# The row of inverse norms: spread over the partitions by way of DRAM instead of by TensorE

## The reference

```python
def rmsnorm(x, g):
    y = x * lax.rsqrt(mean(x * x, -1) + EPS)
    return y * g
x = x + 0.5 * ((silu(rmsnorm(x, g1) @ w_gate) * (rmsnorm(x, g1) @ w_up)) @ w_down)
...
x = rmsnorm(x, final_norm)
# Fox: q, k, v, f_logit, gate = split(x @ w_in)
# log_f = log_sigmoid(f_logit + b_f); cum = cumsum(log_f)
# scores = q k^T * scale + cum_q - cum_k, causal softmax, times v, times silu(gate), @ w_out
```

## Time and profile before

| | |
|---|---|
| time, median of 3 runs | 717.7 us (717.63 to 717.78) |
| profiled execution: its own time | 716.91 us |
| profiled execution: its span | 715.1 us |
| TensorE busy | 704.1 us, 98% |
| VectorE busy | 484.5 us, 68% |
| ScalarE busy | 377.9 us, 53% |
| GpSimd busy | 57.9 us, 8%, 33 instructions |
| granted TensorE clock, mean | 0.998 |

### The profile page before, as it was taken

How to read it: one execution, slowest core, us unless ns; L and a number is a source line. 1 busy time by engine, 2 the same in 40 slices (tenths; PEclk the granted TensorE clock), 3 DMA queues, 4 the chain that set the end, 5 groups by cost and what they waited for, 6 DMA issues and landing times.

```text
span 715.1 us, 9717 instructions
## 1 busy us (share of the span) xinstructions
PE 704.1 (98%) x3724; PEld 595.6 (83%) x3724; DVE 484.5 (68%) x726; ACT 377.9 (53%) x515; POOL 57.9 (8%) x33
## 2 busy tenths in 40 slices
PE   8999999999999999999999999999999999999995
PEld 7888888888887778888888888888888888877884
DVE  5797777755476446777767755566766737798756
ACT  6865545444377645754445644477444624575450
POOL 0000000000001300000000000000006442141001
PEclk9999999999999999999999999999999999999999
DMA  8996555555355323655455555435573183543001
GB/s 292 371 353 260 203 190 176 181 207 201 119 201 210 119 69 138 243 200 203 176 176 185 207 213 222 176 138 216 193 257 133 38 316 125 176 166 124 1 1 59
DMA packets 21731, 129.33 MB, mean 181 GB/s; under 512 B 2584, under 2 KB 4384, under 8 KB 7488
## 3 DMA queue, kind: packets, MB, share of 16 engines
q1 hardware_dynamic: 20160, 127.38, 49.3%
q10 hardware_dynamic: 1488, 1.34, 0.6%
q0 software_dynamic: 48, 0.13, 0.0%
HBM read 127.79 MB, written 1.06 MB: 180 GB/s over the span
## 4 chain that ended last, share of the span: by engine, by line
PE 96%; DVE 1%; ACT 1%; DMA 1%; issue 0%; DVEq 0%; ACTq 0%
PE ps L398 26%; PE ps L378 16%; PE ps L380 15%; PE ps L379 15%; PE ps L402 13%; PE ps L389 1%; PE ps L594 1%; PE ps L937 1%; PE ps L416 1%; PE ps L390 1%; PE ps L766 1%; ACT whi L1011 1%; DMA sm<-in_sm 1%; PE ps L471 0%; PE ps L917 0%; PE ps L927 0%
## 5 line engine op out<-in xcount | busy, mean ns | idle before, releaser
L398 PE MATMUL ps<-xt,whi 128*128 128x512 f32 x796 | 201.3, 393 | 0.0
L1443 DVE TENSOR_TENSOR wlo<-raw,whi 128x2048 fp32r<-128x2048 f32 x69 | 159.0, 2313 | 38.7 <-ACT whi L1011 38.5
L1011 ACT ACTIVATE whi<-raw 128x2048 fp32r<-128x2048 f32 x78 | 148.6, 1908 | 48.9 <-PE ps L380 46.9
L398 PEld LDWEIGHTS ps<-xt,whi 128*128 128x128 f32 x796 | 142.9, 189 | 25.0
L378 PE MATMUL ps<-whi,xt 128*128 128x512 f32 (+1 forms) x304 | 121.9, 401 | 0.1
L380 PE MATMUL ps<-whi,xt 128*128 128x512 f32 (+1 forms) x304 | 117.0, 385 | 0.0
L379 PE MATMUL ps<-wlo,xt 128*128 128x512 f32 (+1 forms) x304 | 116.8, 384 | 0.0
L402 PEld LDWEIGHTS ps<-xt,wlo 128*128 128x128 f32 x796 | 109.1, 190 | 8.0
L402 PE MATMUL ps<-xt,wlo 128*128 128x256 f32 x796 | 111.5, 282 | 0.0
L1396 POOL TENSOR_TENSOR wlo<-raw,whi 128x2048 fp32r<-128x2048 f32 (+1 forms) x9 | 41.3, 4586 | 554.6 <-ACT whi L1011 554.6
L1055 ACT ACTIVATE work<-ps 128x512 f32<-128x512 f32 x44 | 26.2, 597 | 96.8 <-PE ps L398 96.6
(11 more groups left out here) (218 smaller groups left out, 674.4 us busy)
## 6 DMA issues: line engine op xcount, KB each, us to landing
raw<-in_gu SPq DMA_DIRECT2D x41, 1024.0 KB, 4.8
raw<-in_dn SPq DMA_DIRECT2D x22, 1024.0 KB, 4.7
raw<-in_win SPq DMA_DIRECT2D x8, 1024.0 KB, 4.7
raw<-in_fqk SPq DMA_DIRECT2D x8, 1024.0 KB, 4.8
raw<-in_wout SPq DMA_DIRECT2D x4, 1024.0 KB, 5.0
raw<-in_fg SPq DMA_DIRECT2D x4, 1024.0 KB, 4.8
raw<-in_fv SPq DMA_DIRECT2D x4, 1024.0 KB, 4.7
raw<-in_fo SPq DMA_DIRECT2D x4, 1024.0 KB, 4.8
```

Source lines behind the costliest of these rows:

```text
L398: return pe.matmul(ps[:, bank, :], wh[:, w[i]], x, start=ks[i] == 0, stop=ks[i] == KD - 1)
L1011: act.activation(whi[:, c % RING, 0:n], raw[:, c % RING, 0:n], ACT.Copy).then_inc(hi_ready, 1)
L1443: dve.tensor_tensor(wlo[:, c % RING, 0:n], raw[:, c % RING, 0:n], whi[:, c % RING, 0:n].bitcast(F32), ALU.subtract).then_inc(lo_ready, 1)
```

## The change

The diagonals, the products with ones and the copies from PSUM are gone, with all their waits, and the identity's wait on TensorE moves to behind the first pair of chunks. In their place GpSimd waits for the scales, stores them to DRAM as one row of 256 (pieces of 4 bytes, 128 partitions x 2), waits for that store, and reads the row back on all 128 partitions (1 KB each). It does so for the first feed-forward in front of its other work, for the second feed-forward and for Fox behind the chunks of the mixer's output. VectorE waits for the landed row in the places where it waited for the copy, but in both feed-forwards it prepares the second chunk (`lo(C_GU[f] + 1 + RING)`) ahead of the wait and not behind the first hidden product.

```diff
 # TensorE
-            def rstd_to_row(i, bank, diagonal):
-                pe.wait_ge(eye_landed, 16)
-                pe.wait_ge(diag_ready, 2 * i + 2)
-                for t in range(NT):
-                    m = pe.matmul(ps[:, bank, t * P:(t + 1) * P], ones, diagonal[:, t, :], start=True, stop=True)
-                m.then_inc(row_psum, 1)
...
-                            if static and j == 0 and i == 3 and u == 1:
-                                pe.wait_ge(row_ready, f + 1)
...
                 if f == 0:
                     first_pair()
+                    pe.wait_ge(eye_landed, 16)
                 for i in range(2 * (1 - f), 4):
                     gate_and_up(0, i)
-                    if f and i == 1:
-                        rstd_to_row(f, ROW, ffn_diag)
...
-                    if nb and not half:
-                        rstd_to_row(2, 7, diag)
...
                 if h == 1:
                     pe.wait_ge(f_order, 1)
-                    pe.wait_ge(row_ready, 3)
 # ScalarE
-            def row(i, bank, dst):
-                act.wait_ge(row_psum, i + 1)
-                act.activation(dst, ps[:, bank, 0:S], ACT.Copy).then_inc(row_ready, 1)
 # GpSimd
+            def spread_rstd(i, norms, row):
+                pool.wait_ge(rstd_ready, norms)
+                pool.dma_start(rstd_rows[i].rearrange("(t p) -> p t", p=P), rstd, allow_slow_non_contiguous=True).then_inc(rstd_stored, 16)
+                pool.wait_ge(rstd_stored, 16 * (i + 1))
+                pool.dma_start(row, rstd_rows[i].partition_broadcast(P)).then_inc(row_landed, 16)
...
-            for c in [C_WOUT + 1, C_WOUT + 2] + list(range(C_FO, C_DQ)):
+            spread_rstd(0, 1, ffn_row)
+            for c in (C_WOUT + 1, C_WOUT + 2):
+                lo(c)
+            spread_rstd(1, 3, ffn_row)
+            spread_rstd(2, 4, rstd_row)
+            for c in range(C_FO, C_DQ):
                 lo(c)
 # VectorE
-            def diagonal(i, dst):
-                dve.wait_ge(rstd_ready, i + 2 if i else 1)
-                for t in range(NT):
-                    dve.tensor_scalar(dst[:, t, :], ident, rstd[:, t:t + 1], None, ALU.mult).then_inc(diag_ready, 1)
...
                     norm(0)
-                    dve.wait_ge(eye_landed, 16)
-                    diagonal(0, ffn_diag)
                 lo(C_GU[f] + RING)
                 if f:
                     sum_halves(0, 1)
-                dve.wait_ge(row_ready, f + 1)
+                lo(C_GU[f] + 1 + RING)
+                dve.wait_ge(row_landed, 16 * (f + 1))
                 times_row(0, 0)
                 times_row(0, 1)
                 hidden(0, 1, 0)
-                lo(C_GU[f] + 1 + RING)
...
-            dve.wait_ge(row_ready, 3)
+            dve.wait_ge(row_landed, 48)
```

More of the change, by code:

```diff
@@ L64 @@
 N_CHUNKS = C_DO + 4
-DOWN, ROW = 4, 7
+DOWN = 4
 WF_LO = 32
@@ L160, in build @@
         ffn_row = view(work, NG * S + 4 * S, S)
-        ffn_diag = view(work, NG * S + 5 * S, S, "p (t k) -> p t k", t=NT)
         x_turned = view(work, 7700 - KD * S, KD * S, "p (k s) -> p k s", k=KD)
@@ L192, in build @@
         bias2 = gains[:, 1:4, :].rearrange("p a c -> p (a c)").rearrange("p (h k) -> p h k", h=H2)
-        diag = view(work, 6144, 256, "p (t k) -> p t k", t=NT)
         rstd_row = view(work, 6400, 256)
@@ L261, in build @@
             sem(n) for n in ("f_psum", "f_order", "f_neg", "f_soft", "f_log", "cum_ready", "f_rest", "cum_spread"))
-        diag_ready, row_psum, row_ready = sem("diag_ready"), sem("row_psum"), sem("row_ready")
+        rstd_stored, row_landed = sem("rstd_stored"), sem("row_landed")
+        rstd_rows = nc.dram_tensor("rstd_rows", (3, S), F32, kind="Internal").ap()
         gate_ready = sem("gate_ready")
@@ L390, in both_halves, with tile_sums @@
                 return pe.matmul(*small, start=False, stop=False)
-            def tile_sums(bank, wh, wl, u, ks, middle=None):
+            def tile_sums(bank, wh, wl, u, ks):
                 w = [slice(k * S + u * P, k * S + (u + 1) * P) for k in ks]
@@ L404, in tile_sums @@
                     m = high(i)
-                    if middle and i == 2:
-                        middle()
                 return m
@@ L523, in gate_and_up @@
                         for u in range(2):
-                            if static and j == 0 and i == 3 and u == 1:
-                                pe.wait_ge(row_ready, f + 1)
-                            row = (lambda: rstd_to_row(0, ROW, ffn_diag)) if static and j == f == u == 0 and i == 3 else None
-                            m = tile_sums(2 * i + u, wh, wl, u, range(KD), row)
+                            m = tile_sums(2 * i + u, wh, wl, u, range(KD))
                     m.then_inc(chunk_used, 1)
@@ L1068, in ffn @@
                     hi(C_GU[f] + RING)
-                    row(f, ROW, ffn_row)
                     load_table(ACT.Silu)
@@ L1229, in _ @@
                 if nb == 0:
-                    row(2, 7, rstd_row)
                     act.wait_ge(f_psum, 1)
@@ L1679, in _ @@
             norm(2)
-            diagonal(1, ffn_diag)
             dve.wait_ge(wf_hi, 1)
@@ L1690, in _ @@
             norm(3)
-            diagonal(2, diag)
             lo(C_FG + RING)
```

## The result

| | before | after |
|---|---|---|
| time, median of 5 runs each on one chip | 717.63 us (717.51 to 717.78) | 729.04 us (727.56 to 729.77) |
| ratio of the times | | 1.0158, 95% interval 1.0146 to 1.0169 |
| profiled execution: own time / span | 716.91 / 715.1 us | 729.77 / 727.6 us |
| granted TensorE clock, mean | 0.998 | 0.990 |

A forecast was written before the change was run, and what follows sets the result against it. TensorE's own work bounds the kernel (704.1 of 715.1 us busy, 96% of the chain). Removed rows save 0.43 + 0.45 + 0.44 = 1.32 us, everything else counts 0: 717.7 to 716.4 us, range 715.8 to 719.8 us.

The forecast's parts named there:

- What do the two transfers take?: First feed-forward: store and read of the row take 4.1 us each, so the row lands at 33.8 us, no stall.
- The limit: First feed-forward: the row may land as late as 34.5 us, 9.15 us after the scales, without TensorE stalling.
- my bounds: Per transfer, 2.0 us (output stores) to 11.2 us (x loads queued behind other loads); ends: no stall or 13 us.
- Rival A: First feed-forward: store and read each wait for chunk loads ahead; stall 6.3 us, time 722.7 us; chance 0.17.
- Every microsecond beyond T = 34.5 is a microsecond of TensorE: First feed-forward, T being when the row has landed: each microsecond past 34.5 us costs TensorE one microsecond.
- The sign that the prediction named for A or B: First feed-forward: VectorE's first scaling starts after 34.5 us and TensorE idles for the difference behind VectorE's subtraction.
- Rival B: First feed-forward: slower transfers, or GpSimd shut out by VectorE, cause a small stall; 717.9 or 719.0 us; chance 0.17.
- Fox ... 10 us of slack: Fox: row lands at 484.4 us, its first user is needed at 494.5, so TensorE never waits: 0 us.
- what the steps said: Removing the row products saves TensorE 0.43 us (first feed-forward), 0.45 us (second) and 0.44 us (Fox).
- rival C: All three places: each row also broke the weight-load stream; 0.55 us a row, 1.65 us saved, 716.05 us; chance 0.08.
- T + 6.7 us: First feed-forward: chunk 6 is ready for TensorE 6.7 us after the row has landed.
- T may be 306 to 307 us, 18 us after the scales: Second feed-forward: the row may land this late without TensorE stalling; with 8.4 us for the transfers, 0 us.

## Why the prediction was wrong

**The step that failed** is "What do the two transfers take?", and in it the store: "I take 4.1 us for both". The store takes 11.1 to 11.5 us in all three places, the read 6.1 to 6.4. In the first feed-forward that is 17.8 us from scales to row and not 8.4: 7.0 us more for the store, 2.0 for the read, 0.4 for hand-offs. The limit was 9.15 us for everything, so the store alone breaks it. The nearest rows that I chose, the identity and the small parameters, are loads of longer pieces into SBUF; no store of 4-byte neighbours was in the trace, and even the end of my bounds, 11.2 us, was taken from a row with another cause. I held both transfers to the lower part of the bounds with no row for it but likeness, and gave a late row only 0.34 in all. Where the bounds are 2.0 and 11.2 us a transfer and the limit of 4.5 us each lies between them, the chance of a stall was to be taken nearer to a half.

**The Trainium skill.** "DMA: Bandwidth & Descriptors" ("Anatomy of one DMA — SWDGE (gpsimd) path") gives some 2.0 us of fixed cost; here no transfer on GpSimd's queue took less than 3.2 us, and the read alone has a median of 5.5. The same page ("Rules for kernel authors") warns of one descriptor for each element. The warning was right in its sign, and I priced it at nothing. Its ground is not what the runs show: with half as many elements the store took 9.9 to 11.3 us, with as many lying apart 5.6 to 5.9. Its "Specifications" name 512 bytes as the least transfer for full rate; 64-byte pieces took 5.8 us here and 512-byte ones 5.2 (medians), so that bound does not separate the slow stores from the quick ones in this case.

**Rival A** had the right sign and place, and its way to the price ("Every microsecond beyond T = 34.5 is a microsecond of TensorE") holds as far as the idle time goes: TensorE ran out of chunks at 42.57 in this trace, 6.5 us of chain before that is a limit of T = 36.1, and T = 42.86 is 6.8 us beyond it. The slow clock comes on top. The sign that the prediction named for A or B, a late scaling and TensorE idle behind VectorE's subtraction, was there, and yet neither mechanism is the cause. A had the store waiting for the chunk loads that are ahead of it. But beside the same loads in the same place, stores of wider or spaced pieces land in 5.1 to 5.6 us. The store is as slow on ScalarE's queue, too, and in the second feed-forward and in Fox. It is the other way round: the store holds the loads back. It is issued at 25.33 and has landed at 36.4; windows of the kernel after, columns as above (a packet counts whole in the window in which it begins, which is how a share can exceed 1):

```profile
29.00:31.00 2.00, 2.00 (x13) 1.75 (x12) 0.97 (x2) 1.02 (x1) 0.00 (x0) 1.00 2.20 341
31.00:33.00 2.00, 2.00 (x14) 1.82 (x13) 1.35 (x1) 0.00 (x0) 0.00 (x0) 1.00 0.53 33
33.00:35.00 2.00, 2.00 (x14) 1.75 (x13) 0.00 (x0) 0.00 (x0) 0.00 (x0) 1.00 1.20 90
35.00:37.00 2.00, 2.00 (x12) 1.70 (x11) 0.00 (x0) 0.00 (x0) 0.28 (x1) 1.00 0.54 53
...
39.00:41.00 2.00, 2.00 (x14) 1.82 (x13) 0.00 (x0) 0.00 (x0) 0.00 (x0) 1.00 1.03 434
```

Until its pieces are on their way the loads run as ever (410 to 426 GB/s from 25 to 29 us). Then the packets that begin between 29 and 31 us take 2.20 times as long as the window has room for, the last column falls to 33, 90 and 53 GB/s, and it is at 434 behind the store. The 1 MB loads issued while the store is under way (first and second feed-forward) land after more than twice their usual time of about 5 us:

```profile
raw<-in_gu SPq DMA_DIRECT2D x2, 1024.0 KB, 11.5
...
raw<-in_gu SPq DMA_DIRECT2D x2, 1024.0 KB, 11.6
```

In the changed kernel this costs nothing by itself, since four slots lie ahead. With 512-byte pieces in the same place they land in 5.1 and 5.6 us, with pairs in 7.1.

**Rival B.** VectorE did not shut GpSimd out. In the changed kernel it stands idle at 25.33 and 36.72, when GpSimd issues, so that trace can't tell. In the kernel with spaced pieces first the read is issued at 32.32, in the middle of a subtraction of VectorE (31.07 to 33.36); the issue lasts 0.57 us, as it does beside an idle VectorE, and the read lands after 4.4 us, sooner than the 6.1 of the changed kernel. This agrees with what the prediction has from the Trainium skill on `tensor_tensor`.

**The clock** stood in no part of the forecast. In an idle of 6.8 us the granted clock fell to 0.50, and the work behind it took 2.8 us more; without that the first feed-forward would cost 6.4 us and not 9.2.

**"Fox ... 10 us of slack"** failed by the same term: 18.5 us from scales to first use is exactly the limit that it gave (494.5 - 476.0), and TensorE waits 0.87 us there. The 1.75 us behind it I had not looked for: VectorE stands idle for 9.65 us, starts on the forget logits late, and its first sum of a query chunk (line 1700), for which TensorE waits, comes after them and after the subtractions of two chunks.

**What was right.** The rows are worth what the steps said: the second feed-forward gave back 0.45 us between equal instructions, the version with two rows by DRAM 0.9 us, and the one run without a store lies 1.4 us lower. Nothing shows rival C's 0.55 us a row. T + 6.7 us from row to chunk 6 was 6.5. "T may be 306 to 307 us, 18 us after the scales" with no stall in the second feed-forward held, but only just and by luck: 18.1 us were used. GpSimd's own waits held up no one.

**Open.** In every place 1 MB loads run beside the store. No run has the store without them, so whether small neighbouring pieces would be as slow on a quiet core is not shown. The read takes 5.8 to 7.0 us behind a store of small pieces side by side, 4.4 and 5.5 behind the spaced ones, 4.6 to 5.1 (medians) behind wide ones, and 5.5 alone. Loads that were held back run beside it in the first case, but no run separates that. And in the first feed-forward the store of pairs spread from 7.1 to 8.3 us between kernels, for which I have no cause.

## What to carry to other kernels

Price a detour by DRAM as a store plus a read with the latencies of small transfers, from a row with the same piece size and direction. If there is none, take the far end of the bounds and ask whether it still fits ahead of the consumer; here it fitted in two places with pairs, and not in the first. If numbers must be stored one by one, make the pieces wider or put them apart (only the store of spaced pieces was tried here, not reading them back), and keep everything that TensorE needs next, chunks and PSUM banks both, out from behind the wait.

## What the runs showed of the hardware

- Beside a stream of 1 MB loads, a store of 0.5 to 1 KB in 4-byte pieces side by side takes 9.9 to 11.9 us, 256 such pieces 512 bytes apart 5.6 to 5.9, 64 KB in pieces of 512 bytes 5.2 (median). The difference lies behind the store's packets, not in issuing them.
- Once the pieces of such a store are on their way, the DMA engines move 33 to 90 GB/s until it has landed (410 to 426 before), and 1 MB loads issued meanwhile land in 11.5 us.
- During idle times of TensorE of 4.1 and 6.8 us the granted clock fell to 0.50 and stayed there for some microseconds of work; in one of 1.9 us it did not.
